# The first projection of a hybrid decoder step: x loaded in column halves, three bank pairs, page sums of log forgets by scans, forget logits in float32

## The reference, cut to what matters

```python
def ab_inputs(x, hist, norm_g, w_in, b_f, conv_w, q_g, k_g):
    h = rmsnorm(x, norm_g) @ w_in          # 1024 -> 3080 columns
    gb, gc, hv, q, k, v, fl = jnp.split(h, splits, axis=-1)
    ...
    q = rmsnorm(q.reshape(bsz, t, N_HEADS_B, HEAD_DIM), q_g)
    k = rmsnorm(k.reshape(bsz, t, N_HEADS_B, HEAD_DIM), k_g)
    logf = jax.nn.log_sigmoid((fl + b_f).astype(jnp.float32))   # 8 heads
# the sample group attends to 16 cached pages of 128 rows and its own 4 rows:
    lf_all = jnp.concatenate([logf_pool[page_table].reshape(bsz, p_len, h), logf_new], axis=1)
    c = jnp.cumsum(lf_all, axis=1)
    out = fox_attend(q, k_all, v_all, c[:, p_len:], c, q_pos, k_pos)   # logits get c[t] - c[s]
```

## Time and profile before

| | |
|---|---|
| median of 3 runs | 1444.46 us (1442.98 to 1447.14) |
| profiled execution, its own time | 1449.78 us |
| its span, first to last instruction | 1447.9 us |
| PE busy / DVE / ACT / POOL | 96% / 50% / 34% / 44% of the span |
| mean granted TensorE clock | 0.993 |

### The profile page before, as it was taken

The page is one execution under the profiler, slowest core; times in us unless marked ns, Lnnn a source line. Parts: engine busy times, 40 slices in busy tenths (PEclk is TensorE's granted clock), DMA queues, the critical chain, the costliest instruction groups (busy, mean ns, idle before and its releaser), DMA issues. The chain is left out here.

```text
span 1447.9 us, 34492 instructions
## 1 busy us (share of the span) xinstructions
PE 1390.9 (96%) x13989; PEld 1298.6 (90%) x13989; DVE 717.3 (50%) x1226; ACT 487.2 (34%) x718; POOL 630.5 (44%) x401
## 2 busy tenths in 40 slices
PE   6998999998999999999999999979999999999998
PEld 5896777767999999999998977859999999999998
DVE  5645778764345442024442399986454430144411
ACT  4376333332342223122233432236444321222221
POOL 3323455442335554445543544433254554455431
PEclk9999999999999999999999999999999999999999
DMA  6416899978223222332222455532232223332122
GB/s 186 132 54 235 295 355 389 376 249 282 80 65 111 87 72 77 98 102 88 76 63 84 131 149 150 148 102 71 61 100 87 80 77 91 102 88 87 54 84 75
DMA packets 245641, 191.60 MB, mean 132 GB/s; under 512 B 11969, under 2 KB 204946, under 8 KB 245450
## 3 DMA queue, kind: packets, MB, share of 16 engines
q1 hardware_dynamic: 244273, 187.71, 41.8%
q0 software_dynamic: 656, 2.13, 0.5%
q10 hardware_dynamic: 605, 0.24, 0.1%
HBM read 173.03 MB, written 6.04 MB: 124 GB/s over the span
## 5 line engine op out<-in xcount | busy, mean ns | idle before, releaser
L687 POOL TENSOR_TENSOR w_l<-w_raw,w_h 128x1024 fp32r<-128x1024 f32 (+2 forms) x195 | 434.3, 2229 | 401.0 <-ACT w_h L855 387.8
L1838 PE MATMUL banks<-xa_h,w_h 128*128 128x272 f32 x1856 | 388.7, 291 | 4.1 <-DVE tmp L1665 3.3
L1838 PE MATMUL banks<-xa_h,w_l 128*128 128x272 f32 x1856 | 385.3, 289 | 0.0
L1838 PE MATMUL banks<-xa_l,w_h 128*128 128x272 f32 x1856 | 383.9, 288 | 0.0
L1838 PEld LDWEIGHTS banks<-xa_h,w_h 128*128 128x128 f32 x1856 | 293.7, 189 | 6.3 <-issue 5.0
L1838 PEld LDWEIGHTS banks<-xa_l,w_h 128*128 128x128 f32 x1856 | 292.9, 189 | 0.0
L1838 PEld LDWEIGHTS banks<-xa_h,w_l 128*128 128x128 f32 x1856 | 291.1, 190 | 0.0
L855 ACT ACTIVATE w_h<-w_raw 128x1024 fp32r<-128x1024 f32 (+2 forms) x193 | 185.2, 961 | 182.0 <-PE banks L1838 181.9
L1838 PE MATMUL banks<-h_h,w_h 128*128 128x272 f32 x928 | 193.2, 289 | 0.3 <-DVE x L1604 0.3
L1838 PE MATMUL banks<-h_h,w_l 128*128 128x272 f32 x928 | 192.5, 289 | 0.0
L1838 PE MATMUL banks<-h_l,w_h 128*128 128x272 f32 x928 | 191.9, 288 | 0.0
(11 more groups left out here) (302 smaller groups left out, 1668.3 us busy)
## 6 DMA issues: line engine op xcount, KB each, us to landing
w_raw<-in_w_up SPq DMA_DIRECT2D x88, 512.0 KB, 3.6
k_grp<-in_cache_k SPq DMA_DIRECT2D x128, 256.0 KB, 4.8
v_pg<-in_cache_v SPq DMA_DIRECT2D x120, 256.0 KB, 5.5
w_raw<-in_w_in SPq DMA_DIRECT2D x24, 512.0 KB, 6.6
w_raw<-in_w_down SPq DMA_DIRECT2D x32, 384.0 KB, 3.3
w_raw<-in_w_pw SPq DMA_DIRECT2D x24, 512.0 KB, 4.3
w_raw<-in_w_down SPq DMA_DIRECT2D x32, 320.0 KB, 3.2
w_raw<-in_w_out SPq DMA_DIRECT2D x8, 512.0 KB, 5.7
```

Source lines behind the costliest of these rows:

```text
L687: g.tensor_tensor(w_l[:, slot, 0:n], w_raw[:, slot, 0:n], w_h[:, slot, 0:n].bitcast(F32), ALU.subtract).then_inc(s_lo, 1)
L1838: ins = mm(out[:, half, 0:HT], w, v[:, half * HT:(half + 1) * HT], start=first and t == 0 and n == 0, stop=last and t == phase.tiles - 1 a ...
```

## The change

All of it lies in the stage above.

- **x in column halves.** x is loaded as columns 0 to 511, then weight slab 0, then columns 512 to 1023; SP then waits for x before it loads slabs 1 to 3. PE turns chunks 0 to 3 after the first half has landed, 4 and 5 before slab 0, 6 and 7 inside it.
- **Matmuls without use.** PE multiplies `ones` by `ones` 20 times at the start, 16 times behind the first gain and 4 times between chunks 3 and 4 (`kept_awake`).
- **Three bank pairs.** Slabs 0, 1 and 2 go to three different pairs of banks; the sums move to banks 6 and 7.
- **Squares.** POOL squares chunks 0 and 2, ACT the other six; POOL takes the low half of slab 0's weights in two parts and waits for the last square sum before slab 2's low half.
- **Page sums.** `onward` is 1 where a page is the same or a later one of the same group. DVE totals each page's log forgets (`page_totals`), one small matmul adds the pages (`pages_summed`, inside slab 2), and eight scans of 128 elements subtract within the page (`page_decays`), while pages lie on partitions. They come between variance and root on DVE's list. The eight transposes follow them, before slab 3. The 15 additions and the four matmuls of 512 columns are gone.
- **Forget logits.** The gain goes into the forget weights (POOL, `fw_g`), and x itself is multiplied in float32: 8 chunks x 4 column groups of 136 rows, 32 matmuls.

```diff
+SQUARED = (1, 3, 4, 5, 6, 7)
+AWAKE = (20, 16, 4)
...
-        x_turned = [banks[:, n:n + 2, :].rearrange("p k c -> p (k c)")[:, 0:T] for n in (0, 4, 2, 6)]
+        x_turned = [banks[:, n:n + 2, :].rearrange("p k c -> p (k c)")[:, 0:T] for n in (0, 4, 2, 6, 0, 2, 6, 0)]
+        sides = banks[:, 6:8, :]
+        idle_bank = banks[:, 1, 256:256 + P]
+        qkv_out = lambda n: (pair[1], pair[0], psum_s)[n] if n < 3 else pair[n % 2]
...
+            x_half(0)
...
             for j in range(4):
                 load(ph["qkv"], 0, j, cols(w_in, 1536 + j * P))
+                if j == 0:
+                    x_half(1)
...
+                    sp.wait_ge(s_xld[1], 16 * 5)
```

On POOL:

```diff
+            pool.wait_ge(s_hi, 1)
+            for at, signal in ((slice(0, 512), s_lo0), (slice(512, DC * P), s_lo)):
+                g.tensor_tensor(w_l[:, 0, at], w_raw[:, 0, at], w_h[:, 0, at].bitcast(F32), ALU.subtract).then_inc(signal, 1)
+            split_low(0, 1, DC)
             pool.wait_ge(s_ix, 16)
             g.indirect_dma_start(out=lf_pg[:, :], out_offset=None,
...
-            pool.wait_ge(s_xlo, DC)
-            for slot in range(1, 3):
-                split_low(0, slot, DC)
-            pool.wait_ge(s_fw, 33)
-            g.tensor_tensor(fw_l[:, :, :], fw[:, :, :], fw_h[:, :, :].bitcast(F32), ALU.subtract).then_inc(s_fw, 1)
+            for b in range(2):
+                pool.wait_ge(s_xlo, 2 * b + 1)
+                g.tensor_tensor(tmp[:, b, :], x[:, 2 * b, :], x[:, 2 * b, :], ALU.mult).then_inc(s_sqe, 1)
+            pool.wait_ge(s_ss, 9)
+            split_low(0, 2, DC)
...
+            g.tensor_tensor(fw_g[:, :, :], fw[:, :, :], params[:, 0:DC].unsqueeze(2).to_broadcast([P, DC, NH]), ALU.mult)\
+             .then_inc(s_fw, 1)
             for n in range(9):
                 split_low((n + 3) // 4, (n + 3) % 4, DC)
```

On ACT the list per chunk becomes (chunk m of 8):

```diff
-                if m == 1:
+                if m == 0:
                     split_high(0, 0, DC)
+                if m == 3:
+                    A(r_all[:, 0:1], ones[:, 0:1], ACT.Ln).then_inc(s_ln0, 1)
+                if m == 5:
+                    split_high(0, 1, DC)
```

On DVE:

```diff
+            def page_totals():
+
+                dve.wait_ge(s_lf, 16)
+                V.tensor_reduce(onward_sum, by_head, AX.X, ALU.add).then_inc(s_suf, 1)
+
+            def page_decays():
+
+                dve.wait_ge(s_misc, 3)
+                V.tensor_copy(from_page, sides[:, 0, 0:NH]).then_inc(s_miscd, 1)
+                dve.wait_ge(s_miscd, 3)
+                for h in range(NH):
+                    V.tensor_tensor_scan(dk_page[:, h, :], ones[:, :], by_head[:, h, :], from_page[:, h:h + 1], ALU.mult,
+                                         ALU.subtract).then_inc(s_decay, 1)
...
+            dve.wait_ge(s_sqe, 2)
+            V.tensor_tensor(ssum[:, :], tmp[:, 0, :], tmp[:, 1, :], ALU.add).then_inc(s_ss, 3)
...
+            for n in range(len(SQUARED)):
+                if n == 4:
+                    params_kept()
+                dve.wait_ge(s_sq, n + 1)
+                dve.wait_ge(s_ss, n + 3)
+                V.tensor_tensor(ssum[:, :], ssum[:, :], sq[:, n % 2, :], ALU.add).then_inc(s_ss, 1)
+            page_totals()
+            inv_rms(0, 0, sides, page_decays)
...
-                if n == 1:
-                    later_sums()
                 if n == 2:
                     selectors()
+                    decays()
```

On PE:

```diff
-            pe.wait_ge(s_cst, 15)
+            pe.wait_ge(s_cst, 2)
+            kept_awake(AWAKE[0])
+            pe.wait_ge(s_cst, 16)
             pe.wait_ge(s_gin, 16)
             tr(bank[0][:, 0:DC], p_rows[0:DC, 0, :], ident[0:DC, 0:DC]).then_inc(s_gn, 1)
+            kept_awake(AWAKE[1])
+            pe.wait_ge(s_xld[0], 16 * 5)
...
+                if k == 6:
                     pe.wait_ge(s_ss, 9)
+                    pe.wait_ge(s_miscd, 2)
+                    sum_channels(sides)
...
+                if k == 3:
+                    pe.wait_ge(s_var, 1)
+                    pe.wait_ge(s_suf, 1)
+                    mm(sides[:, 0, 0:NH], onward[:, :], onward_sum, start=True, stop=True).then_inc(s_misc, 1)
...
-                pe.wait_ge(s_fw, 34)
+                pe.wait_ge(s_fw, 33)
+                pe.wait_ge(s_xnew, DC)
                 for t in range(DC):
-                    for n, (w, v) in enumerate(((fw_h, xa_h), (fw_h, xa_l), (fw_l, xa_h))):
-                        for half in range(2):
...
+                    for c in range(4):
+                        ins = mm(bank[0][32 * c:32 * c + NH, 0:QT], fw_g[:, t, :], x[:, t, c * QT:(c + 1) * QT],
+                                 start=t == 0, stop=t == DC - 1)
...
-                if n == 1:
+                if n == 2:
+                    pe.wait_ge(s_decay, NH)
                     for h in range(NH):
...
                 if n == 3:
-                    pe.wait_ge(s_miscd, 3)
-                    pe.wait_ge(s_suf, 1)
...
+                    pe.wait_ge(s_miscd, 5)
                     forget_gate()
```

More of the change, by code:

```diff
@@ L21 @@
 HT = T // 2
+QT = T // 4
 NH, HD = 8, 64
@@ L196, in build @@
         causal, _ = place("causal", [P, P], F32)
-        later, _ = place("later", [P, P], F32)
+        onward, _ = place("onward", [P, P], F32)
         params, _ = place("params", [P, n_rows], F32)
@@ L263, in build @@
         cq = small[:, 160:192]
+        onward_sum, from_page = small[:, 216:224], small[:, 152:160]
         cns = small[0:TS, 192:200]
@@ L1242, in _ @@
[L1242 to L1251, removed]
@@ L1825, in slab @@
                 s, g = phase.slab(i, j), phase.group(i, j)
-                pe.wait_ge(s_lo, s + 1)
+                if phase is order[0] and s == 0:
+                    pe.wait_ge(s_lo0, 1)
+                else:
+                    pe.wait_ge(s_lo, s + 1)
                 if first:
                     bank_free(phase, i, j // phase.per_group, g)
-                out = pair[(j // phase.per_group) % 2]
+                out = qkv_out(s) if phase is order[0] else pair[(j // phase.per_group) % 2]
                 for t in range(phase.tiles):
@@ L1866, in bank_free, with sum_channels, kept_awake @@
                 else:
                     pe.wait_ge(s_xnew if phase.residual else s_free, g - 1)
-            def sum_channels():
+            def sum_channels(dst=psum_s):
                 for half in range(2):
-                    ins = mm(psum_s[:, half, 0:HT], ones[:, :], ssum[:, half * HT:(half + 1) * HT], start=True, stop=True)
+                    ins = mm(dst[:, half, 0:HT], ones[:, :], ssum[:, half * HT:(half + 1) * HT], start=True, stop=True)
                 ins.then_inc(s_stat, 1)
-            pe.wait_ge(s_cst, 15)
+            def kept_awake(n):
+                for _ in range(n):
+                    mm(idle_bank, ones[:, :], ones[:, :], start=True, stop=True)
@@ new lines, in chunk_turned @@
+            def chunk_turned(m):
+                free = {4: 1, 5: 3, 6: 4, 7: 5}.get(m)
+                if free:
+                    pe.wait_ge(s_xlo, free)
+                    pe.wait_ge(s_xhi, free)
+                for t in range(4):
+                    tr(x_turned[m][:, t * P:(t + 1) * P], x_rows[:, t, m * P:(m + 1) * P], ident[:, :])
+                tr(x_turned[m][:, TP:T], x_rows[0:TS, 4, m * P:(m + 1) * P], ident[0:TS, 0:TS]).then_inc(s_tp, 1)
+            pe.wait_ge(s_cst, 2)
+            kept_awake(AWAKE[0])
@@ L1890, in _, with first_chunks @@
-            pe.wait_ge(s_xlo, 5)
+                chunk_turned(m)
+            pe.wait_ge(s_xlo, 1)
+            pe.wait_ge(s_xhi, 1)
+            kept_awake(AWAKE[2])
+            pe.wait_ge(s_xld[1], 16 * 5)
+            for m in range(4, 6):
+                chunk_turned(m)
+            def first_chunks(k):
+                if k in (3, 4):
+                    chunk_turned(k + 3)
+                if k == 4:
+                    pe.wait_ge(s_lo, 1)
+                pe.wait_ge(s_xlo, k + 1)
             def params_turned():
@@ L1937, in _ @@
-                    for half in range(2):
-                        at = slice(half * 512, half * 512 + 512)
-                        mm(psum_s[:, half, :], later[:, :], lf2[:, at], start=True, stop=False)
-                        ins = mm(psum_s[:, half, :], ones[:, :], suf2[:, at], start=False, stop=True)
-                    ins.then_inc(s_misc, 1)
+                    pe.wait_ge(s_miscd, 5)
                     forget_gate()
```

157 lines of the change are left out of this document (74 added, 83 removed).

## The result

The changed kernel takes 1457.03 us (median of 9 runs, 1450.24 to 1463.28), the kernel before beside it 1447.14 (9 runs, 1442.27 to 1449.92). The ratio is 1.0067, 95% interval 1.0041 to 1.0094: 0.67% slower, about 9.7 us. In a later comparison, with runs of its own, it was 1.0061 (1.0040 to 1.0082). The forecast was 1445.9 us, range 1434 to 1450: the time lies above the range.

The account below looks back on a forecast made before the run. Bound taken: a queue on PE. Last square sum 35.6 + scans 16.5 + transposes 2.1 + slab 3 7.6 + forget logits 2.0 = 63.8 against 62.42 us, so 1444.46 + 1.4 = 1445.9 us, range 1434 to 1450.

Parts of the forecast that it names:

- what moves the mark moves the end by as much: Everything behind slab 4's first matmul is the same and led by PE, so 1.4 us later there means 1.4 later overall.
- the mark: First matmul of slab 4 in the first projection: 62.42 us before, 63.8 forecast.
- Start: First x transpose at 11.8 us (11.5 to 12.8), 2 later than before, behind 36 `ones` matmuls; half of x lands about 5.8.
- Chunks: x transposes at the high clock, led by ACT: slab 1's weight copy ends at 21.3 us, slab 0 near 25.5, 2.4 earlier.
- Square sums: DVE's last square-sum addition, with its waits on POOL, ends at 35.6 us (33.76 before); PE waits over 4 us.
- Scans: Eight DVE scans, four held by POOL's four halves, end 16.5 us behind the last square sum (8.1 to 17.7); PE waits 7.9.
- Behind the scans: Between scans and slab 4: eight transposes 2.1 us, slab 3 7.6, forget logits 2.0 with four column groups side by side.
- Rivals: Four alternatives in the first projection: scans not held (0.36), fewer POOL halves meeting scans (0.10), no clock rise or serial column groups (0.09 together).
- the free scans: Rival: POOL does not hold the scans before slab 3; slab 4 starts at 53.3 us, 9.1 earlier, run 1435.4; chance 0.36.
- The clock did rise at the start: Rival denied this: first chunk's transposes at 19.2 us, everything behind 7.4 later, run 1453.3; 0.09 shared with serial column groups.

Follow-up runs that it names:

- the place alone: Kernel before with 182 PE instructions put ahead of its first transposes, so its attention starts elsewhere within the 256-instruction pieces: 1454.75 us, ratio 1.0052.
- places 198 to 250: PE instructions ahead of attention, modulo 256: 227 kernel before, 1447.14 us; with POOL held off the scans, 198 (44 more), 1436.72; 250 (`ones` matmuls left out), 1439.11.
- 153, 154 and 96: Same count: 153 kernel before plus 182 PE instructions, 1454.75 us; 154 changed kernel, 1457.03; 96 changed kernel with POOL held and 198 more instructions, 1464.82.
- experiment 5: Changed kernel with POOL held off the scans and attention moved back to 227 modulo 256, its 40 `ones` matmuls shrunk to 32 rows by 8 columns by 1: 1432.62 us.
- the second profile: Changed kernel run once more, unaltered: 1452.33 us, ratio 1.0061, attention 245.6 us.
- Experiment 2: Changed kernel with POOL's low half of slab 3 held until the eight scans end: 1448.93 us; with attention also moved back to 227 modulo 256: 1444.02.
- the changed kernel moved back: Changed kernel with 73 PE instructions (18 tiny matmuls, waits already met) added at the start, returning attention to 227 modulo 256: 1449.22 us, ratio 1.0008.

## Why the prediction was wrong

The step that failed stands in its first part: "everything behind it is the same in both kernels", so "what moves the mark moves the end by as much". The work behind the mark is the same, but not where it lies in PE's stream of instructions. The change puts 183 more PE instructions ahead of the attention, 160 of them for the matmuls of `ones`. Of the profiled attention's extra 9.5 us (248.04 against 238.51, cut alike at its first matmul and at the first transpose behind it), stops at ends of pieces are 6.9 - 1.8 = 5.1. The rest fits the clock: the granted clock was 0.97 over this stage and 0.99 before, as the trace has it at the low level (1.2 GHz) for 17.1 us and before for 4.0; 13.1 us at half pace lose up to 6.5 (estimate). Only part of that comes from the stops. Right behind the two longest of them, from 179.1 and 209.8 on, it is low for 6.8 us together; but from 127.9 on it is low for 6.8 us behind waits for DVE and ACT at the stage's start, which the kernel before has too, without a fall. So the loss by the place in this execution is 5.1 us of stops and up to 3.4 of clock. The first of these two falls (windows of 10 us that hold and follow the first stop):

```profile
170.00:180.00 10.00, 7.33 (x170) 5.94 (x169) 8.83 (x15) 2.83 (x4) 2.08 (x3) 0.96 1.07 383
180.00:190.00 10.00, 10.00 (x109) 8.94 (x108) 5.08 (x11) 2.63 (x8) 7.43 (x12) 0.87 0.61 200
```

In the medians, the later start of the attention, 1.2 us, and the place alone, about 7.5 (ratio 1.0052 in the kernel before), make 8.7 of the 9.7, and the intervals are wider than what is left.

The Trainium skill (Runtime: NRT & Kernel Launch, Instruction fetch mechanics) says that instructions come in blocks of 16 KiB, 256 each, while the block before is executed, and that crossing a block's end is mostly hidden. The block size agrees with the 16.4 KB and 256 records here. The crossing is hidden at places 198 to 250, where stops add up to 0.6 to 3.4 us, and not at 153, 154 and 96, where they add up to 6.5 to 18.6 us.

Point by point:

- *Start:* first transpose at 11.51 (11.8 taken, 11.5 to 12.8); slab 0's pairs at 0.41 from 19.79 on. Right. The trace's records of the clock begin with its rise to 2.4 GHz, at 5.04 us here, at 24.14 in the kernel before and at 21.44 with the small matmuls of experiment 5; the 1.00 that windows show ahead of that, in the earlier trace rows too, only says that no record stands there. That x's half waits for PE was right too, though not by how much: it is there at about 7.8 and not 5.8 (by the start of the transposes at 7.86 in experiment 5; half of x is 1.11 MB, not 1.09, which makes 0.1 us of it). The matmuls of `ones` are what kept it waiting, some 4 us.
- *Chunks:* slab 0 ended at 27.14 where 25.5 was worked out. The sum had one table load for ACT. Before, one stood in the idle start (7.69) and none at the copies behind it; now there are two of 1.28 us, one ahead of the first copy (12.39) and one ahead of the logarithm (18.20). So slab 1's weight copy ended at 22.37, not 21.3. With the later slab 0 the wait for the square sums was 2.3 us, not over 4.
- *Square sums:* the last one ended at 34.98 (35.6). Right to 0.6 us.
- *Scans:* they started at 41.89, 6.9 us behind it (5.3), and POOL at 41.24, 6.3 behind it (6.6). So POOL came first; four scans lasted 2.03 to 2.60 us beside one half each, the other four 0.45, and the end was 17.9 us behind the last square sum (16.5, and 17.7 as the upper bound, for which no sum is given). The number of scans held, four, and the wait, 7.4 us (7.9), were right. In the second profile three scans had begun before POOL did, four were held, and one followed. Experiment 2 shows the cause: the same eight take 3.21 us without POOL. The rule of the Trainium skill (SBUF — State Buffer, Who interferes with whom) gives the forecast's sum, and the trace agrees: 2.03 to 2.60 us for a scan beside a half, 0.45 for one without.
- *Behind the scans:* transposes 1.97 us (2.1), slab 3 6.94 (7.6), forget logits 2.05 (2.0, so the four groups do run side by side). Right. That the mark came to 0.3 us is partly luck: the scans' end lay 1.4 us further behind the last square sum than worked out, while the square sums, the transposes (1.68 us from the scans' end to slab 3) and slab 3 came out 1.7 us shorter together.
- *Rivals:* the free scans were built in experiment 2: mark 55.2 (53.3 worked out, PE's new wait of 1.2 us for POOL included in the 55.2). The clock did rise at the start. None of the rivals was what happened, and none lay behind the mark.

The rows of the second and third point, ACT's and DVE's timelines:

```profile
12.39 1.28 ACT L924 ACT_TABLE_LOAD   x1 [12.39 <-PE banks L1933]
18.20 1.28 ACT L928 ACT_TABLE_LOAD   x1
```
```profile
33.44 1.54 DVE L1301 TENSOR_TENSOR ssum<-ssum,sq 128x544 f32<-128x544 f32 x2
```

What stays open: the stretch behind the attention took 1078.7 to 1089.5 us in the profiles, without a tie to the place (at 227: 1078.7 to 1088.7) and without a stop of over 0.5 us at the end of a piece. In four of the five longest of the fourteen DVE is busy for 480 to 485 us there, in the nine shorter ones for 451 to 471; the fifth, the changed kernel moved back (1087.3), has 459. The two kernels' rows further up are an example. It was short in both profiles of the changed kernel (1080.4 and 1080.2 cut alike), which hides most of its loss in its profiled execution; but other versions of it reach 1087 to 1089.5, and the medians of 9 and 11 runs don't show that advantage. It was not followed up.

## What to carry to other kernels

An edit moves all that is listed behind it on its engine through the pieces in which instructions arrive, and where 256 PE instructions pass in under 3 us beside heavy transfers this decides over several us. So before a small difference is put down to an edit, look for waits named issue, and compare with a copy in which instructions that cost nothing move the place. A chain of short two-input DVE instructions is to be kept clear of POOL's long ones, even if a slab's low half starts 3 us later for it.

## What the runs showed of the hardware that was not expected

- PE's instructions share the DMA engines with the data: a piece's transfer started 3.05 and 3.23 us after the point counted from with 315 and 318 GB/s moving in the attention, 1.0 us with 145 GB/s. PE went on 1.2 us after the transfer's end at the earliest.
- A shift of PE's stream by 58 instructions modulo 256 (154 to 96) moved the attention by 9.8 us, from 252.0 to 261.8, at the same work.
- 40 matmuls that raise the clock ahead of the transposes cost more than they give: without their work slab 0 starts 3.1 us earlier at half pace, and slab 4 3.5 us earlier.
